# Front steps and routes placed by a table of loads; gelu taken of the masked weights, one weight product per pair

## The reference, cut to what matters

```
n  = rmsnorm(x, g_mix) * (1 + sc1) + sh1
z  = n @ w_in                                  # 4096 columns: a_lin, a_gate, u, v, g_a, g_b
a  = silu(layernorm(causal_dwconv(a_lin * sigmoid(a_gate)))) @ w_conv_out   # 31 taps
b  = (u * chunk_spatial_gate(layernorm(v))) @ w_gmlp_out
x  = x + gt1 * ((sigmoid(g_a) * a + sigmoid(g_b) * b) @ w_out)
n2 = rmsnorm(x, g_ffn) * (1 + sc2) + sh2
# peer, for each row and each of 8 heads: two top-16 of 128 key scores, then the top 16 of their sums
eid, g = 128 expert numbers per row, their softmax weights
act = gelu(u_tab[eid] . n2)                    # one dot product of 1024 per expert
x   = x + gt2 * sum(g * act * v_tab[eid])
y   = rmsnorm(x, g_final)
```

## Time and profile before

| | |
|---|---|
| median of three runs | 3511.39 us (3509.34 to 3520.03) |
| profiled execution, its own time | 3523.17 us |
| its span in the trace | 3521.6 us |
| granted TensorE clock, mean over the span | 0.707 |
| busy: TensorE matmul, VectorE, ScalarE, GpSimd | 2047.3, 2446.7, 440.0, 1230.9 us |
| instructions | 28830 |
| first gelu of the peer stage | 305.6 us |

### The profile page before, as it was taken

The page is one execution under the profiler, slowest core; times in us unless marked ns, Lnnn a source line. Parts: engine busy times, 40 slices in busy tenths (PEclk is TensorE's granted clock), DMA queues, the critical chain, the costliest instruction groups (busy, mean ns, idle before and its releaser), DMA issues. The chain is left out here.

```text
span 3521.6 us, 28830 instructions
## 1 busy us (share of the span) xinstructions
PE 2047.3 (58%) x9548; PEld 993.7 (28%) x9548; DVE 2446.7 (69%) x6290; ACT 440.0 (12%) x1031; POOL 1230.9 (35%) x1046
## 2 busy tenths in 40 slices
PE   6873878987267767688678733333333333355333
PEld 4762534544044445355345400000000000000000
DVE  1447575479898887655768997787868678556665
ACT  1121101011111201110211010011010101010200
POOL 0001211222223433234444433444444444434433
PEclk9886979998579879799789855555555555555555
DMA  7744756698669999899999977999999999998998
GB/s 298 303 158 155 298 208 259 265 353 316 244 259 356 384 309 369 333 370 419 416 403 407 381 291 320 421 422 421 419 421 422 421 415 402 419 404 347 422 423 342
DMA packets 183925, 1232.08 MB, mean 350 GB/s; under 512 B 30512, under 2 KB 31152, under 8 KB 36320
## 3 DMA queue, kind: packets, MB, share of 16 engines
q0 software_dynamic: 148608, 1082.20, 76.4%
q1 hardware_dynamic: 35168, 148.05, 10.8%
HBM read 1221.14 MB, written 9.02 MB: 349 GB/s over the span
## 5 line engine op out<-in xcount | busy, mean ns | idle before, releaser
L1047 POOL DMA_INDIRECT big<-in_experts,eid x920 | 1096.4, 1192 | 2071.1 <-PE ps L767 1613.0
L1509 DVE SCALAR_TENSOR_TENSOR big<-big,xr 128x1024 f32<-128x1024 f32 x920 | 1113.7, 1224 | 504.1 <-DMA big<-in_experts,eid 498.8
L767 PE MATMUL ps<-big,wd 128*32 128x512 f32 x3680 | 724.0, 871 | 1067.0 <-DVE wd L1526 1065.0
L532 PE MATMUL ps<-big,wring 128*128 128x260 f32 (+2 forms) x2400 | 646.4, 423 | 81.4 <-issue 56.2
L532 PEld LDWEIGHTS ps<-big,wring 128*128 128x128 f32 x2400 | 447.6, 201 | 320.7 <-issue 170.9
L767 PEld LDWEIGHTS ps<-big,wd 128*32 128x32 f32 x3680 | 84.9, 127 | 1569.2 <-DVE wd L1526 1523.6
L989 ACT ACTIVATE gel<-act 128x2 f32<-128x2 f32 x516 | 104.8, 203 | 2535.0 <-DVE big L1509 2295.6
L1526 DVE TENSOR_SCALAR wd<-mask,gel,gate 128x32 f32<-128x32 f32 x1024 | 277.9, 363 | 154.1 <-ACT gel L989 143.5
L767 PE MATMUL ps<-w,wd 128*32 128x512 f32 x208 | 100.3, 1061 | 166.4 <-DVE wd L1526 162.5
L1207 DVE SCALAR_TENSOR_TENSOR arena<-arena,wdw 128x128 f32<-128x128 f32 (+2 forms) x360 | 182.6, 565 | 0.0
L684 PE MATMUL ps<-wring,mbuf 128*128 128x256 f32 (+1 forms) x528 | 125.8, 394 | 11.4 <-DMA wring<-in_w_out 6.5
(11 more groups left out here) (219 smaller groups left out, 1873.7 us busy)
## 6 DMA issues: line engine op xcount, KB each, us to landing
wring<-in_w_in SPq DMA_DIRECT2D x40, 1024.0 KB, 10.2
wring<-in_w_q SPq DMA_DIRECT2D x19, 1024.0 KB, 9.1
big<-in_experts,eid POOLq DMA_INDIRECT x920, 11.8
wring<-in_w_ada SPq DMA_DIRECT2D x12, 1024.0 KB, 7.4
wring<-in_w_out SPq DMA_DIRECT2D x9, 1024.0 KB, 9.7
big<-in_w_ada SPq DMA_DIRECT2D x6, 1024.0 KB, 7.2
xr<-in_w_ada SPq DMA_DIRECT2D x6, 1024.0 KB, 8.8
big<-in_w_in SPq DMA_DIRECT2D x4, 1024.0 KB, 14.7
```

Of the source, the lines that this page charges most:

```text
L532: mm = mmul(out, piece(n)[:, c, col:col + P], src[:, c, gi * tg:(gi + 1) * tg], start=(c == 0), stop=(c == k - 1))
L767: mm = mmul(ps[QUAD * j:QUAD * (j + 1), half, :], wd[:, 2 * (at % 4) + jj, :], row(2 * slot + jj)[:, D + 512 * h:D + 512 * (h + 1)], start ...
L1047: gp.indirect_dma_start(row(r), None, t["experts"], bass.IndirectOffsetOnAxis(ap=index, axis=0)).then_inc(s_row[r], 16)
L1509: last = v.scalar_tensor_tensor(out=row(r)[:, 0:D], in0=row(r)[:, 0:D], scalar=1.0, in1=x, op0=ALU.mult, op1=ALU.mult, accum_out=act[:, c: ...
```

## The change

The group starts stay 0, 1 and 4, the buffers stay six and then ten row tiles, and the plan of who uses which buffer comes out the same, now kept by tile instead of by pair. Constants such as 512, `GW` and "group 3" become expressions. What differs in the program that runs:

- `front_weights` and `spread_front` go. Each step has a load in us for TensorE and one for VectorE. `place_steps` goes through the pairs with a budget: each pair may take `pace` us on each engine, less 1.6 (TensorE) or 3.0 (VectorE) for the pair itself; unspent budget is kept up to two pairs' worth. The smallest pace that fits all steps is taken.
- The later routes' pieces come from the same budget. Until all are placed, the next group's front stops at `limit = head - 8`.
- VectorE's loads are shifted by four steps against TensorE's, and TensorE's norm has one step of gap more before it and one less behind.
- `gelu`: ScalarE takes the gelu of mask x dot product, 128x32 for each of the two tiles, straight into `wd`, and waits for `rows_used` (from the fifth pair on) in VectorE's place. `weigh`: VectorE multiplies both tiles by their gates in one 128x64 product. The sample's four pairs stay as they were.

```diff
-HEAVY = 3
-END_B = 60
-END_C = 4 * PAIRS - 8
+PE_BASE, DVE_BASE = 1.6, 3.0
+ROUTE_LOADS = [1.6, 1.6, 3.9, 3.6, 5.5, 5.5, 5.5, 8.4, 0.7, 3.5]
...
+        def front_loads(g):
+            tg, ng, nb = g.tg, g.ng, g.nb
+            mm, op, tap = 4 * max(0.4, 0.0021 * tg), 0.15 + 0.0007 * tg, (0.3 + 0.0012 * g.np) * taps_per_step[g.n]
+            light = (0.1, 0.1)
+            head = [*norm_loads(g), *[light] * 5, *[(mm, op / 4)] * (4 * CC * ng), *[light] * 5]
+            steps = head + [(mm, tap)] * (2 * CC * ng) + [light] * 5
+            steps += [(2.2, tap / 2 + 0.7)] * (4 * nb) + [(0.1, 0.5)] * 12 + [(0.8, tap + 0.9)] * (2 * nb) + [light] * 5
+            steps += [(mm, tap + op / 3)] * (3 * KC * ng) + [light] * 5 + [(0.2, 0.6)] * 19
+            steps += [(mm, 2 * op / 3)] * (3 * KC * ng) + [light] * 7 + [(2.2, 0.43)] * (8 * nb) + [light] * 3
+            steps += [*norm_loads(g), *[light] * 5, *[(1.4, 0.1)] * (2 * nb), *[light] * 3]
+            per = 2 * ng + 1
+            top = 1.7 * g.nf / per
+            q = 2 * mm * ng / per
+            steps += [(q, 0.1)] * (3 * per) + [(q, top)] * (per * (NCH - 3)) + [(0.1, top)] * (3 * per) + [light] * 4
+            if g.n == LAST:
+                steps += [(0.1, 2.2 / ng)] * (8 * ng)
+            steps += [(0.1, 0.6)] * 9 + [(0.1, d) for d in ROUTE_LOADS] + [light]
+            late = 4
+            return [(pe, dve) for (pe, _), (_, dve) in zip(steps + [light] * late, [light] * late + steps)], len(head)
...
         def spread_front():
+            for g in GROUPS[1:]:
+                lo, hi = PAIRS * STARTS[g.n - 2], PAIRS * STARTS[g.n - 1] - (4 if g.n < LAST else 8)
+                loads, head = front_loads(g)
+                routes = ROUTE_LOADS * len(later_turns(before[g.n]))
+                found, pace = None, 5.2
+                while found is None:
+                    pace += 0.05
+                    found = place_steps(loads, head, routes, lo, hi, pace)
...
             def gelu(at):
                 c = 2 * (at % 4)
+                if at >= 4:
+                    act_.wait_ge(S["rows_used"], at - 3)
                 act_.wait_ge(S["dots"], at + 1)
-                ac(gel[:, c:c + 2], act[:, c:c + 2], ACT.Gelu).then_inc(S["gelu"], 1)
+                if place(at)[0] is None:
+                    last = ac(gel[:, c:c + 2], act[:, c:c + 2], ACT.Gelu)
+                else:
+                    for jj in range(2):
+                        last = ac(wd[:, c + jj, :], mask[:], ACT.Gelu, scale=act[:, c + jj:c + jj + 1])
+                last.then_inc(S["gelu"], 1)
...
             def weigh(at):
                 b, half, m = place(at)
                 dve.wait_ge(S["gelu"], at + 1)
-                if at >= 4:
-                    dve.wait_ge(S["rows_used"], at - 3)
...
-                        last = v.tensor_scalar(wd[:, c, :], mask[:], gel[:, c:c + 1],
-                                               gate[:, b % 4, 2 * half + jj, m:m + 1], ALU.mult, ALU.mult)
+                    last = v.tensor_tensor(wd[:, c:c + 2, :], wd[:, c:c + 2, :],
+                                           gate[:, b % 4, 2 * half:2 * half + 2, m:m + 1].broadcast_to([P, 2, QUAD]), ALU.mult)
```

More of the change, by code:

```diff
@@ L355, in spread_front @@
-        def spread_front():
[L357 to L367, removed]
@@ new lines, in later_turns @@
+        def later_turns(g):
+            return [(g, turn) for turn in range(1, g.nb)]
+        def spread_front():
+            steps, pieces = [(None, 0)] * NPAIRS, []
+            for g in GROUPS[1:]:
[6 more added lines that the diff above has]
+                    found = place_steps(loads, head, routes, lo, hi, pace)
+                for at, (count, piece) in found.items():
+                    steps[at] = (g.n, count)
+                    pieces += [at] if piece else []
+            rest = ROUTE_PIECES * (GL.nb - 1) + 1
+            each = (SAMPLE_AT - 8 - WIDE_AT) // rest
+            pieces += [WIDE_AT + each * i for i in range(rest)]
+            return steps, pieces
@@ new lines, in build @@
+        taps_per_step = {g.n: -(-CC * W // (2 * CC * g.ng + (4 * g.nb if g.n >= 2 else 0) + 3 * KC * g.ng))
+                         for g in GROUPS}
+        front_steps, route_pieces = spread_front()
+        last_step = {g.n: max(at for at in range(NPAIRS) if front_steps[at][0] == g.n) for g in GROUPS[1:]}
+        routing, first = [], 0
+        for g in GROUPS:
+            for _, turn in later_turns(g):
+                routing.append((g, turn, first))
+                first += ROUTE_PIECES + (g.blocks[g.order[turn]] == NB)
@@ L443, in _ @@
                 if n == 16:
[L444 to L453, removed]
+                    bring_x(GROUPS[1])
@@ new lines, in _ @@
+            for g in GROUPS[1:-1]:
+                for n in range(first_piece[g.n], first_piece[g.n + 1] + (3 if g.n == LAST - 1 else 0)):
+                    if n == first_piece[g.n] + 4 and g.n < LAST - 1:
+                        bring_x(GROUPS[g.n])
+                    with_spill(n, g)
+            ahead = before[LAST]
+            sp.wait_ge(*ahead.to("oa_mm", KC * ahead.ng))
+            sp.wait_ge(*ahead.to("s_done", NCH))
+            sp.wait_ge(*ahead.to("sq_act", 1))
+            sp.wait_ge(*ahead.to("tables", 1))
@@ L748, in value @@
                 b, half, m = place(at)
-                slot = PLAN[at][0]
+                rows = [row(tile[0]) for tile in PLAN[at]]
                 pe.wait_ge(S["weights"], at + 1)
@@ L788, in begin @@
                         made[0] += 1
-            beside_peer(begin, value, {2: front(G2), 3: front(G3)}, lambda at: None, share=0.5)
+            beside_peer(begin, value, {g.n: front(g) for g in GROUPS[1:]}, lambda at: None, share=0.5)
         @block.scalar
@@ L1620, in _ @@
             dve.wait_ge(S["mask_made"], 1)
-            beside_peer(dots, weigh, {2: front(G2), 3: front(G3)}, extra)
+            beside_peer(dots, weigh, {g.n: front(g) for g in GROUPS[1:]}, extra)
             take_acc(2 * NB)
```

313 lines of the change are left out of this document (161 added, 152 removed).

## The result

The changed kernel takes 3528.22 us (median of 7 runs, 3525.12 to 3532.76) against 3511.39 us, a ratio of 1.0049 [1.0036, 1.0063]: **slower by 17 us**, where 14 us less was forecast. The time lies inside the range given, but on the slower side of the kernel before. Its profiled execution took 3530.74 us, its span is 3529.2 us (3521.6 before).

A forecast was written before the change was run, and what follows sets the result against it. Front matmuls bound part A, DMA and VectorE alternately part B, gathers part C. With -10 us in B, -4 in A and zero for the rest, 3511.4 us becomes 3497 us, range 3450 to 3550.

The forecast's parts named there:

- ScalarE's wait for `rows_used`: Ahead of gelu, for the pair four back: costs nothing up to pair 255, as value is done long before.
- The masked activation: Between dots and weigh: two 128x32 activations of about 0.22 us each, the chain 0.22 to 0.4 us longer.
- net saving in an exposed pair: Pairs without a step between dots and weigh: only about 0.1 us of the product's 0.32 us saved.
- branch A and `w_out`: Part B: 44 pairs become 35.4, TensorE 207.5 us plus slack 9 gives 216 us (257 before).
- line 1's slack: Part B's first stretch, norm, gate and lin with later routes: 6 us of slack within 250 us for 38.7 pairs.
- The routes' 24 pairs: Pairs 64 to 87, G2's later routes with only 22 front steps: VectorE 156 us, TensorE almost idle.
- the -10: Part B's change in us, taken between -21 (stretch's pairs lend freely) and +23 (no pair lends).
- the stage sum's 1213: Part B summed over ten stretches, pairs lending freely: 1213 us against 1234, 21 us less.
- Part A: Pairs 0 to 63, bound mostly by front matmuls: -4 us taken, between +3 by stretches and -16 pair by pair.
- pair-by-pair end: Part A with each pair taken by itself: 619 us before, 603 after, -16, as eleven-step and nine-step pairs go.
- The slower one: Rival: front matmuls become part B's bound, +23 us there, A at best -4, half clock 5: 3535 us; chance 0.25.
- Evenness paying in full: Rival: A gains 16 us, B 21, C 5, and slack from unequal pairs another 5: 3464 us; chance 0.27.

The follow-up runs named there:

- e5: Kernel before with the new gelu and weigh, plus an unused one-column gelu carrying the rows_used wait ahead of the dots wait: 3488.91 us, 0.9940.
- e2: Kernel before with only the changed gelu and weigh, old placement: 3514.93 us, 0.9999.
- e4: Kernel before with the new gelu and weigh, weight buffer five pairs deep, no rows_used wait on ScalarE: 3494.81 us, 0.9945.
- e6: Changed kernel with the weight buffer five pairs deep and no rows_used wait on ScalarE: 3511.86 us, 0.9991 against the kernel before.
- e1: Changed kernel with the old gelu and weigh, so the new placement alone: 3523.36 us, 1.0027 against the kernel before.
- e3: Kernel before with only the new list of G2's front steps for pairs 0 to 59: 3518.28 us, 1.0010.
- e7: Kernel before with G3's norm steps at pairs 64 to 68, none at 69 to 87, the rest spread later by old weights: 3538.08 us, 1.0072.
- e9: Kernel before with G3's steps spread by the new table and budget, no route charged, nothing held back, routes as before: 3518.34 us, 1.0011.
- e8: Kernel before with VectorE multiplying mask and gates ahead of the dots, the old 128x2 gelu, then one 128x64 product: 3491.47 us, 0.9934.

## Why the prediction was wrong, point by point

**The wait on ScalarE: the step that failed.** The prediction said that ScalarE's wait for `rows_used` "costs nothing up to pair 255", and looked for TensorE being late. TensorE is not late: e5 keeps the wait and loses nothing by it. What costs is its place: the gelu then has two waits, its table load, which had run ahead of the one wait, stands behind the dots, and it starts 0.06 us later in every pair. From the ratios of e2, e4 and e5 this is 19 to 21 us, and 20 from the changed kernel and e6: more than the whole measured loss. The trace of before has 23 such loads, with 0.4 us of idle time ahead of them in all; they stood in a row of their own that the prediction didn't read, and it counted no table load at all. The line of the groups, from before:

```profile
L989 ACT ACT_TABLE_LOAD x23 | 29.5, 1283 | 0.4
```

**The masked activation was mis-sized.** The estimate of 0.22 us was interpolated between forms without a column as an operand. It measures 0.313, two of them 0.53, against 0.203 for the old one. The Trainium skill, "ScalarE: Activation LUTs", "What ACT_TABLE_LOAD costs", has the term that was missed: 186 ns + 0.833 ns an element, and about 93 ns more for each operand that is a [128,1] pointer. That makes an estimated 306 ns for this form. The trace agrees (313), and so does its 1283 ns for a load. The net saving in an exposed pair, put at +0.1 us, is -0.07 us (0.32 saved, 0.39 more waiting), and -0.01 with one wait.

**The product, and the rule weighed against it.** 0.224 us and VectorE's total at 2294 us (2283 forecast) are right. The products' busy time fell by 163 us, 0.32 a pair. The prediction's other estimate, 0.12 us a pair by the Trainium skill, "VectorE: DVE Perf Modes", would be 61 us, so the rows decided rightly. With one wait ahead of the gelu (e4) the new weights are worth 0.55% [0.38, 0.72], 19 us: about an eighth of the 163 arrives. It does not come only from the pairs beside routes and norms, where the prediction saw VectorE as the bound: in e4's trace pairs 64 to 87 take 4.9 us less than before, pairs 233 to 255 2.1 less, and the 145 pairs between them 15.6 less.

**Part B, pair counts and stretches.** The forecast counts of pairs came out to within one (36 pairs for branch A and `w_out`, forecast 35.4; 27 for q, forecast 26.7), and five of the stretch times within 9 us: 90, 68, 28, 50 and 155 us were forecast as 89, 68, 32, 50 and 164. Gate and lin took 96.6, forecast 94 with line 1's slack. Three failed. The routes' 24 pairs took 171.6 instead of 156: VectorE's work is 145.6, below what was counted, but it stands idle for 26 us, 17.0 of them for ScalarE (a wait of 0.66 us or more in most of these pairs, where 0.22 was put). Branch B took 160.5 instead of 154. Branch A and `w_out` took 231.9 instead of 216, although TensorE was busy for 206.6, as summed: the slack of 9 us had been taken from a stretch that the gathers bounded. Once TensorE bounds it, the time that TensorE waits counts in full: 25 us, of which 14.3 are a single wait whose releaser the profile doesn't name (the kernel before has one of 14.1 in its stretch), 6.7 are for a weight piece and 3.0 for a pair's weights. The changed kernel's part B came out 10 us above before, in the other half of the range from the -10 that was taken. With new weights and no second wait (e6) it is 1224.5 us in its trace, with old weights (e1) 1234.4: even for e6 the stage sum's 1213 is too low by 12. That e6's trace shows just the -10 is luck, since its median is level with before.

**Part A.** -4 was taken; e1, e3 and the changed kernel show none (632.0, 1.0010, 630.3). Pooled over a stretch it was +3, and that was nearer: the pair-by-pair end of -16 is refuted (e3, at best 1 us faster).

**Part C** was put at zero: +2.4 us in the trace of the changed kernel, within what traces differ by. Right.

**The rivals.** The slower one named the right mechanism for the placement: fewer matmuls beside the routes, TensorE as the later bound, q at 5.8 us a pair. It priced part B at 23 us; e7 gives 25 for the hold-back alone, e1 10 for the placement as planned. Its sign, over 5.9 us a pair in branch A or q, came in branch A and `w_out` (6.4). It did not name the table load or the second wait, without which the changed kernel is level with before (e6): its 3535 us is near the measured 3528 partly by luck. Evenness paying in full is refuted by e3 and e9. (The range's lower end has a slip: that rival with its slack doubled is 3459 us, not 3450. Nothing hangs on it.)

**The signs that were asked for.** Pair 64 came at 931.3 us (925 to 940 said). Pairs 64 to 87 took 7.15 us each at a clock of 0.52 (6.5 and 0.5 to 0.6 said), pair 256 came at 2176.0 (2145 to 2165 said), q's pairs took 5.8 us (6.0 to 6.4 said) with TensorE 99% busy but the DMA share at 0.99 (below 0.9 said). The prediction called itself wrong "if the two ScalarE activations take over 0.3 us each and are waited for", and that came.

## What to carry to other kernels

When a wait is moved to ScalarE, look at the activation behind it: if its function's table has been replaced since, count the load, and make sure that something which needs the same table comes ahead of the long wait, or that the activation has only one wait. Work taken off an engine is worth only a part of its busy time (here an eighth), less what the chain between two engines grows; a shorter chain with a third of the work taken away (e8) gained as much as all of it with a longer chain (e4). Placing steps by a budget gave nothing here where it took apart work that had overlapped: TensorE's idle stretch beside the routes was paid for by its later steps.

## What had not been expected of the hardware

A load of a table (1.283 us) ran before a wait when its activation had one wait, and after it when there were two: 0.4 us of idle time ahead of 23 loads (e4) against 152.8 us (e2), which differ in that wait and in the depth of the weight buffer. The second wait also started the activation 0.06 us later where there was no load. An activation with a [128,1] column as its scale took 0.313 us for 32 elements where one of 2 elements without it took 0.203. Two of them in a row took 0.53 us, so they overlapped by 0.1 us.
